# Attention rounds of a decoder layer in a new order: weighted sums first, splits before maxima, exponentials a round later

## What is computed

```python
s = einsum(q, kc) * scale;  pc = softmax(where(cvalid, s, NEG)) ;  o_cmp = pc @ vc        # 16 compressed blocks
s2 = einsum(q, k_selected) * scale; p2 = softmax(where(kpos <= pos, s2, NEG)); o_slc = p2 @ v_selected
s = einsum(q, k_win) * scale; p = softmax(where(in_window, s, NEG)); o_win = p @ v_win    # window of 512 and own block
o_att = g0 * o_cmp + g1 * o_slc + g2 * o_win
```

## Time and profile before

| | |
|---|---|
| timed runs, median | 2830.82 us |
| the profiled execution | 2830.15 us, span 2828.5 us |
| the prompt's attention, first scores to the last split | 1123.8 to 1445.6 us, 321.8 us |
| mean granted TensorE clock, whole span | 0.945 |
| engines busy over the span | TensorE 90%, GpSimd 42%, VectorE 35%, ScalarE 23% |

### The profile page before, as it was taken

The page is one execution under the profiler, slowest core; times in us unless marked ns, Lnnn a source line. Parts: engine busy times, 40 slices in busy tenths (PEclk is TensorE's granted clock), DMA queues, the critical chain, the costliest instruction groups (busy, mean ns, idle before and its releaser), DMA issues.

```text
span 2828.5 us, 50789 instructions
## 1 busy us (share of the span) xinstructions
PE 2554.1 (90%) x20106; PEld 1741.1 (62%) x20106; DVE 975.9 (35%) x1440; ACT 662.5 (23%) x1438; POOL 1194.0 (42%) x885
## 2 busy tenths in 40 slices
PE   7999999999969898866675999999969999999997
PEld 3666666666649854554443666666636666666665
DVE  2322222311085433866532442222172223232104
ACT  3311111101052243755430011111251111111002
POOL 2378787834333330100022884444334434443431
PEclk9999999999989955999997999999989999999998
DMA  6133333321102431000033332211101111121111
GB/s 233 38 97 95 97 95 98 100 62 41 50 8 54 146 99 36 2 1 1 1 97 100 104 101 57 55 45 56 46 15 54 51 52 52 45 60 52 51 31 60
DMA packets 298368, 179.52 MB, mean 63 GB/s; under 512 B 8847, under 2 KB 288773, under 8 KB 298176
## 3 DMA queue, kind: packets, MB, share of 16 engines
q1 hardware_dynamic: 282780, 156.15, 18.9%
q0 software_dynamic: 3840, 11.54, 1.4%
q10 hardware_dynamic: 11620, 10.04, 1.1%
HBM read 170.81 MB, written 11.10 MB: 64 GB/s over the span
## 4 chain that ended last, share of the span: by engine, by line
PE 74%; issue 13%; DVE 6%; ACT 3%; POOL 2%; DMA 1%; SPq 0%; POOLq 0%; ACTq 0%; DVEq 0%
PE banks L224 23%; PE banks L225 23%; PE banks L226 22%; PE banks L1481 2%; ACT pair L521 1%; DVE rs L577 1%; PE banks L320 1%; ACT ahi L524 1%; PE banks L2217 1%; DVE y L594 1%; POOL orow L1865 1%; POOL opart L1862 1%; DVE pair L617 0%; PE banks L461 0%; DVE alo L607 0%
## 5 line engine op out<-in xcount | busy, mean ns | idle before, releaser
L224 PE MATMUL banks<-ahi,whi 128*128 128x344 f16 x2784 | 865.9, 311 | 26.9 <-ACT sg L876 14.4
L225 PE MATMUL banks<-alo,whi 128*128 128x344 f16 x2784 | 865.8, 311 | 0.0
L226 PE MATMUL banks<-ahi,wlo 128*128 128x344 f16 x2784 | 865.7, 311 | 0.0
L215 POOL TENSOR_SCALAR stage<-stage 128x1024 f32<-128x1024 f32 (+1 forms) x248 | 273.6, 1103 | 975.3 <-PE banks L226 907.0
L220 POOL TENSOR_TENSOR wlo<-stage,whi 128x1024 f16<-128x1024 f32 (+1 forms) x248 | 545.8, 2201 | 20.6
L224 PEld LDWEIGHTS banks<-ahi,whi 128*128 128x128 f16 x2784 | 273.8, 98 | 165.2 <-issue 16.2
L226 PEld LDWEIGHTS banks<-ahi,wlo 128*128 128x128 f16 x2784 | 273.9, 98 | 136.5
L225 PEld LDWEIGHTS banks<-alo,whi 128*128 128x128 f16 x2784 | 273.9, 98 | 133.4 <-issue 0.4
L224 PE MATMUL banks<-hhi,whi 128*128 128x344 f16 x1056 | 326.3, 309 | 3.2 <-DVE hlo L937 3.2
L225 PE MATMUL banks<-hlo,whi 128*128 128x344 f16 x1056 | 326.3, 309 | 0.0
L226 PE MATMUL banks<-hhi,wlo 128*128 128x344 f16 x1056 | 326.3, 309 | 0.0
(11 more groups left out here) (320 smaller groups left out, 3765.8 us busy)
## 6 DMA issues: line engine op xcount, KB each, us to landing
stage<-in_w_ffn_gu_dram SPq DMA_DIRECT2D x88, 512.0 KB, 3.9
stage<-in_w_ada_dram SPq DMA_DIRECT2D x56, 512.0 KB, 3.8
stage<-in_w_ffn_down_dram SPq DMA_DIRECT2D x32, 704.0 KB, 4.7
stage<-in_w_in_dram SPq DMA_DIRECT2D x38, 512.0 KB, 3.8
first<-in_w_ada_dram SPq DMA_DIRECT2D x4, 2048.0 KB, 12.8
xrow<-in_x_prompt_dram ACTq DMA_DIRECT2D x8, 512.0 KB, 7.1
stage<-in_phi_w_dram SPq DMA_DIRECT2D x8, 512.0 KB, 3.8
ring<-in_state_win_kv_dram SPq DMA_DIRECT2D x16, 256.0 KB, 3.3
```

The lines of the kernel that those rows point to most:

```text
L215: pool.tensor_scalar(st, st, WS, 1.0, ALU.mult, ALU.mult).then_inc(slab_scaled, 1)
L224: pe.matmul(out, w_hi, a_hi, start=start, stop=False)
L225: pe.matmul(out, w_hi, a_lo, start=False, stop=False)
L226: return pe.matmul(out, w_lo, a_hi, start=False, stop=stop)
```

## The change

It reorders the calls in a round and moves the compressed unit by one round behind the others:

- TensorE: weighted sum of u-4, scores of u, turn of u-2; a compressed unit is turned in its third round and weighted in its fifth.
- VectorE: pair of u-5, low split of u-3, maximum of u; the compressed shares come after the maximum of two rounds on.
- ScalarE: high split of u-3, exponentials of u-1 instead of u.
- The row's turn comes one round later (`RL` 5 for 4).
- `greatest` waits for the exponentials of unit u-4 by name instead of by a count. `exponent`, `score_unit`, `turn_bank` and the buffers stay.

```diff
-                    if u >= 4:
-                        dve.wait_ge(S("p_exp"), at("p_exp") - 2)
+                    if u - 4 in prob_ready and units[u - 4][0] != "cmp":
+                        dve.wait_ge(S("p_exp"), prob_ready[u - 4][1])
                     dve.reduce_max(stat[:, u % 4:u % 4 + 1], scores(u), AX_X, negate=True).then_inc(S("s_max"), 1)
...
-        RL = 4
+        RL = 5
         for u in range(U + PL + RL + 2):
-            def unit(back):
-                return u - back if 0 <= u - back < U else None
+            def unit(back, compressed):
+
+                v = u - back
+                return v if 0 <= v < U and (units[v][0] == "cmp") == compressed else None
...
-            if unit(0) is not None:
+            if unit(PL, False) is not None:
+                weighted(u - PL)
+            if u < U:
                 score_unit(u)
-            if unit(TL) is not None:
+            if unit(TL, False) is not None:
                 turn(u - TL)
-            if unit(PL) is not None:
-                weighted(u - PL)
+            if unit(TL + 1, True) is not None:
+                turn(u - TL - 1)
+            if unit(PL + 1, True) is not None:
+                weighted(u - PL - 1)
             if row_end(PL + RL) is not None:
                 rows_turn(row_end(PL + RL))
-            if unit(PL + 1) is not None and units[u - PL - 1][0] == "win" and units[u - PL - 1][2] % 2 == 1:
-                pair_shares(u - PL - 1)
-            if unit(0) is not None:
-                greatest(u)
-            if unit(EV) is not None:
+
+            if unit(EV, False) is not None:
                 turned_hi(u - EV)
-            if unit(PL + 1) is not None and units[u - PL - 1][0] == "cmp":
-                compressed_row(units[u - PL - 1][1])
+            if unit(EV + 1, True) is not None:
+                turned_hi(u - EV - 1)
+            if unit(PL + 2, True) is not None:
+                compressed_row(units[u - PL - 2][1])
             if row_end(PL + RL + 1) is not None:
                 rows_hi(row_end(PL + RL + 1))
-            if unit(0) is not None:
-                exponent(u)
-            if unit(1) is not None and units[u - 1][0] == "cmp":
-                compressed_shares(u - 1)
-            if unit(EV) is not None:
+
+            v = unit(PL + 1, False)
+            if v is not None and units[v][0] == "win" and units[v][2] % 2 == 1:
+                pair_shares(v)
+            if unit(EV, False) is not None:
                 turned_lo(u - EV)
+            if u < U:
+                greatest(u)
+            if 1 <= u <= U:
+                exponent(u - 1)
+            if unit(2, True) is not None:
+                compressed_shares(u - 2)
             if row_end(PL + RL + 1) is not None:
                 rows_lo(row_end(PL + RL + 1))
```

## The result

The changed kernel takes 2871.02 us (median, 2869.35 to 2871.99) against 2829.84 for the kernel before on the same chip: a ratio of 1.0145 [1.0127, 1.0163], slower by 1.5%. The profiled execution took 2870.71 us, its span is 2869.0, 40.5 more than before, at a mean granted clock of 0.936 (before 0.945). Outside attention nothing moved: the stage's last split now ends at 1485.64 instead of 1445.56, which is 40.1 of those 40.5.

What follows compares the result with a forecast made beforehand. Before, VectorE bound t=3, and from t=4 a loop through scores, maximum, split, second turn group and weighted sum. Terms +9.4, +38.4, -4.0, -5.3 and +2 make +40 on 2830.15: 2870 us, range 2852 to 2902.

Steps and rivals of the forecast that it cites:

- the ring: Attention: exponentials, high split, low split, next maximum in series each round, as exponentials wait one maximum extra; 2870 us, chance 0.78.
- The ring's price: Round as sum of its four durations: 2.65 us at t=3, 3.09 to 3.65 for t=4 to 7.
- The compressed unit: Rounds around it open the ring, saving net 0.6 to 3.3 us per t for t=1 to 7.
- the rival that made it larger: Around compressed units the ring opens for more rounds, saving another 14 us: 2856, chance 0.04.
- The low clock: TensorE, idling in each round, falls to half clock for t=0 to 3: +30 us, 2900, chance 0.13.
- a sign against it: A granted clock near half through t=0 to 3 would put the excess on the scores, not the ring.
- The rival's price of about 1 us: At half clock, rounds where TensorE's weighted sum waits for the pair lengthen by about 1 us.
- the price of a normal round: At half clock, scores no longer fit beside the two splits: 0.3 to 0.5 us more per normal round.
- The first mark: Exponentials of head 7's selected unit at t=0 were to come 9.4 us later than before.
- the drain: Last units, from the final t=7 exponentials of head 7's selected unit to the last split: 9.6 us, 14.9 before.
- The 2 us given back for the low clock: Half of some 4 us that a half-clock stretch at t=7 cost the kernel before: +2.
- The rival of the own count: Exponentials wait only for their own maximum, no ring; from t=4 VectorE's work sets 2.2 us rounds: 2760, chance 0.05.

Runs made afterwards that it cites:

- the first experiment: The changed kernel with one number altered: the exponentials of u-1 wait for their own unit's maximum, not for all maxima issued so far; 2770.16 us, ratio 0.9783.
- the doubled turns: The changed kernel with every transposition of a weights tile done twice on TensorE, 536 matmuls more; 2864.15 us, ratio 1.0112.

## Why the prediction held, and where it didn't

The forecast was 2870 us, the time is 2871.02. That they agree within about 1 us is luck: the terms below miss by up to 2 us each, in both directions. **The mechanism** was right: in the profiled execution no E(u-1) starts before M(u) ends, H, L and M follow each other as forecast, and the first experiment takes the ring away with one number. The split done twice puts 0.62 us of work on the ring and gets 0.63 back in the round.

**The ring's price.** Forecast 2.65 a round at t = 3, measured 2.62; 3.27 at t = 5 in the mean over the two kinds, measured 3.30 and 3.19 by turns. The handoffs do cancel. (At t = 0 the forecast's own terms add up to 1.41 a round, not 1.39; over ten rounds that is 0.2 us.)

**The compressed unit.** At t = 3, from 1212.06 to 1220.61 four rounds take 8.55 us where four of 2.62 would be 10.48: 1.9 saved, forecast 1.6. With the doubled turns, at the full clock, the same step is 41.9 us, which is 17 x 2.62 - 2.6. So the saving was undersized by about 1 us at t = 3, and the rival that made it larger had a small part in it. The walk itself held at t = 5, which it was made for: the four rounds took 10.8 us for 10.15.

**The low clock** came as its rival said, at t = 0 to 3, with 0.51 to 0.92 granted, but not all through and not for 30 us; at t = 0 it stood near half, which the forecast had named as a sign against it. Its size can be estimated from the doubled turns, where the clock was higher: 3.7 us at t = 1 to 3 and 2.8 at t = 4 to 7, if the added work itself cost nothing. The rival's price of about 1 us where W waits for the pair is seen in single rounds, 1.5 us in the one at t = 7. What it had too large is the price of a normal round: at t = 3 thirteen rounds ran at 2.63 us in the mean, with the clock at 1.00 in the window of 1218 to 1245 and at 0.83 behind it, where one round of 2.74 is the longest. The swing between the levels of which the Trainium skill, "TensorE: Matmul & The Clock Gate", Part 1, tells is there in these windows, 0.51 to 1.00; a price that decides isn't. And 108.8 against 108.7 for t = 1 to 3 is in part two errors that cancel: the ring's steps would be 105.1 without the low clock, as far as that run can stand for it.

**Start and end.** The first mark came 7.2 us later (forecast 9.4), the drain took 11.7 us (forecast 9.6). Both terms were sums of short durations without a row of their own, and they missed by 2 us in opposite directions. The 2 us given back for the low clock from t = 4 on are near the 2.8 of the doubled turns.

**The rival of the own count** was worked out at 2760 and measures 2770.16 once the wait is made so. Its t = 4 to 7 came out near what was worked out: 155.4 us, or 2.29 a round, against 2.2. The larger part of the miss is at t = 0 to 3, where it was said that nothing changes: the first mark is 3.1 us later (1141.88), and the next three steps take 77.5 us instead of 70.3. What the rival left out is W at the head of TensorE's round, waiting for the pair with the next scores behind it: with W behind the turn the first mark is at 1137.96 and the three steps take 69.8 us, and nothing of the excess is left. A part of it at t = 0 and 1 may be the clock, 0.64 and 0.83 in the first experiment and 1.00 and 0.91 there; at t = 3 both have 1.00, and the step is 29.7 against 26.7 us.

The Trainium skill, "Perfetto Trace Analysis", Optimization Strategy, says that a gap that repeats on the engine that should be saturated can mean too few buffers. The runs bear out half of it: the second turn group's gap went when the turn banks came free earlier, with the same three banks in another order; but the change's own repeating gap, 1.36 us before each E at t = 3, is no lack of a buffer, and a wait that names the right event removes it (over t = 4 to 7 the exponentials into `prw` wait 2.4 us for maxima in the first experiment, 49.6 in the change).

## What to carry to other kernels

A wait written as "all that have been counted so far" changes its meaning when a call moves past another: when you reorder issue order, write down for every wait which event it names, and follow that event back through both in-order queues until you come to the waiting instruction again. Price such a ring as the sum of its steps' durations, and test it with two doses: longer work on it must be paid in full, longer work beside it not. An order that opens one ring is good only with the order of the queues it leans on: here, split first needs the later exponential, the later exponential needs its own count, and weighted sums first need split first, and even then pay only from t = 4 on. Two runs with the same total can differ at every stage, so compare the stages.

## What was not expected of the hardware

- More work on TensorE went with a slightly faster kernel: 536 transpositions more, and 2864.15 instead of 2871.02 us (the runs are 2862.37 to 2865.65 and 2869.35 to 2871.99, not measured side by side; in the traces the steps of t = 1 to 7 are 6.5 us shorter in all). In the same stretch, 1176 us to about 1212, TensorE was busy 24.79 of 35 us with the doubled turns at a granted clock of 1.00, and 23.94 of 36 us without them at 0.87.
- One wider wait on ScalarE lowered TensorE's clock: with it in the kernel before, the windows of t = 4 to 7 have granted clocks of 0.65 to 0.76, and without it 0.92 to 1.00. At t = 5 TensorE is busy 54.0 of 93 us with it (clock 0.65) and 33.9 of 54 without (0.97).
